# A delta-rule level product that moves all 128 columns, and a few places changed in the projections' order

## What is computed

```python
qkv, z, beta_raw, a_raw = jnp.split(h @ w_in, ...)
conv = sum over 4 taps of xp[:, j:j + T] * conv_w[j]
qkv = jax.nn.silu(conv)
q = _l2norm(q) * (DK ** -0.5);  k = _l2norm(k)
beta = jax.nn.sigmoid(beta_raw)
a = -jnp.exp(a_log) * jax.nn.softplus(a_raw + dt_bias)
b = jnp.cumsum(ac, axis=-1)
L = einsum(kc, kc) * exp(where(strict, diff, -inf)) * bc[..., :, None]
rhs = concatenate([vc * bc, kc * (bc * exp(b))])
sol = triangular_solve(L + eye, rhs, lower, unit_diagonal)
```

## Time and profile before

| | |
|---|---|
| median of 3 runs | 2790.02 us (2787.69 to 2792.81) |
| the profiled execution, own time | 2788.71 us |
| its span | 2787.1 us |
| TensorE busy (matmul) | 2654.8 us, 95% |
| VectorE, ScalarE, GpSimd busy | 1267.6, 823.5, 299.5 us |
| mean granted TensorE clock | 0.966 of full |
| chain that ended last | 86% TensorE, 7% VectorE, 3% ScalarE |

### The profile page before, as it was taken

How to read it: one execution, slowest core, us unless ns; L and a number is a source line. 1 busy time by engine, 2 the same in 40 slices (tenths; PEclk the granted TensorE clock), 3 DMA queues, 4 the chain that set the end, 5 groups by cost and what they waited for, 6 DMA issues and landing times.

```text
span 2787.1 us, 48986 instructions
## 1 busy us (share of the span) xinstructions
PE 2654.8 (95%) x20689; PEld 2550.1 (91%) x20689; DVE 1267.6 (45%) x1589; ACT 823.5 (30%) x1047; POOL 299.5 (11%) x307
## 2 busy tenths in 40 slices
PE   7999999999999999999999999989989898999997
PEld 6999998888879899999999999879988898999997
DVE  4444334636364654442344433474446645444323
ACT  3222222323232432222322222233423333322222
POOL 1000001202020210000100000004410342000000
PEclk8999999999999999999999999998899989999998
DMA  4332233424242433322433323211111111333231
GB/s 121 92 90 81 77 101 116 178 76 178 77 178 77 144 87 92 92 73 84 112 91 90 90 73 93 93 61 49 39 57 64 33 46 35 91 90 90 72 93 62
DMA packets 340961, 246.80 MB, mean 89 GB/s; under 512 B 9540, under 2 KB 322044, under 8 KB 340832
## 3 DMA queue, kind: packets, MB, share of 16 engines
q1 hardware_dynamic: 326480, 197.32, 24.1%
q0 software_dynamic: 14352, 47.58, 4.7%
HBM read 218.81 MB, written 26.05 MB: 88 GB/s over the span
## 4 chain that ended last, share of the span: by engine, by line
PE 86%; DVE 7%; ACT 3%; issue 3%; DMA 0%; POOL 0%; SPq 0%; DVEq 0%; POOLq 0%; ACTq 0%
PE ps L733 57%; PE ps L917 13%; PE ps L1103 3%; PE ps L1126 2%; PE ps L815 1%; ACT wh L1305 1%; PE ps L1113 1%; DVE wl L1610 1%; PE ps L1045 1%; PE ps L1056 1%; PE ps L824 1%; DVE cv L1929 1%; PE ps L770 1%; PE ps L1068 0%; PE ps L836 0%
## 5 line engine op out<-in xcount | busy, mean ns | idle before, releaser
L1610 DVE TENSOR_TENSOR wl<-raw,wh 128x2048 fp32r<-128x2048 f32 (+1 forms) x204 | 427.5, 2095 | 338.0 <-ACT wh L1305 337.9
L733 PE MATMUL ps<-xh,wh 128*128 128x260 f32 x2816 | 569.4, 283 | 4.9 <-DVE gate L2153 4.4
L733 PE MATMUL ps<-xh,wl 128*128 128x260 f32 x2816 | 568.6, 284 | 0.0
L733 PE MATMUL ps<-xl,wh 128*128 128x260 f32 x2816 | 567.7, 283 | 0.0
L1305 ACT ACTIVATE wh<-raw 128x2048 fp32r<-128x2048 f32 (+1 forms) x204 | 354.5, 1738 | 347.4 <-PE ps L733 212.0
L733 PEld LDWEIGHTS ps<-xh,wh 128*128 128x128 f32 x2816 | 435.9, 189 | 6.5 <-issue 5.2
L733 PEld LDWEIGHTS ps<-xh,wl 128*128 128x128 f32 x2816 | 435.4, 189 | 0.0
L733 PEld LDWEIGHTS ps<-xl,wh 128*128 128x128 f32 x2816 | 434.1, 189 | 0.0
L733 PE MATMUL ps<-hh,wh 128*128 128x260 f32 x1408 | 287.5, 286 | 13.5 <-DVE hl L2158 13.5
L733 PE MATMUL ps<-hl,wh 128*128 128x260 f32 x1408 | 285.5, 285 | 0.0
L733 PE MATMUL ps<-hh,wl 128*128 128x260 f32 x1408 | 285.4, 284 | 0.0
(11 more groups left out here) (349 smaller groups left out, 3005.5 us busy)
## 6 DMA issues: line engine op xcount, KB each, us to landing
raw<-in_ffn_gu_dram SPq DMA_DIRECT2D x176, 512.0 KB, 5.0
raw<-in_ffn_down_dram SPq DMA_DIRECT2D x64, 384.0 KB, 3.7
raw<-in_ret_w_in_dram SPq DMA_DIRECT2D x48, 512.0 KB, 4.5
raw<-in_ffn_down_dram SPq DMA_DIRECT2D x64, 320.0 KB, 4.1
s_ring<-in_state_ret_dram POOLq DMA_DIRECT2D x32, 512.0 KB, 6.5
out_dram<-s_ring POOLq DMA_DIRECT2D x32, 512.0 KB, 3.1
raw<-in_gdn_w_in_dram SPq DMA_DIRECT2D x32, 512.0 KB, 4.6
raw<-in_ret_w_out_dram SPq DMA_DIRECT2D x16, 512.0 KB, 4.2
```

Of the source, the lines that this page charges most:

```text
L733: m_ = nc.tensor.matmul(ps[:, 2 * q + h, 0:HALF], w_, v[:, kt0 + t, h * HALF:(h + 1) * HALF], start=b_, stop=e_)
L1610: nc.vector.tensor_tensor(wl[:, s, 0:cols], raw[:, s, 0:cols], wh[:, s, 0:cols].bitcast(F32), ALU.subtract).then_inc(w_low, 1)
```

## The change

Five edits, all in the delta-rule mixer. (1) `change` multiplies all 128 columns of `t1`, not the odd blocks alone, through the helper `four`; what VectorE reads of it stays the same. (2) GpSimd clears both `t1` tiles once per group, after cse2 and ahead of the stores of the conv state, so that the columns never written hold zeros. (3) The length of the eighth square (ln7) stands after unit 8 rather than 9, behind ln6, and ScalarE's root before si9 rather than behind it. (4) The product of the token decays (bcol, blast) stands after unit 6 rather than 5. (5) ScalarE's first weights split of a group stands before its wait for the turned conv state.

```diff
-LENGTH_AFTER = {n: n - 2 for n in range(2, 10)}
+LENGTH_AFTER = {**{n: [n - 2] for n in range(2, 8)}, 8: [6, 7]}
...
-    "ctc", each(4, "si", "sq"), "si4 cse0 sq4 si5 sq5 si6 sq6 si7 sq7 si8 cse1 si9 rt si10 si11 cse2",
+    "ctc", each(4, "si", "sq"), "si4 cse0 sq4 si5 sq5 si6 sq6 si7 sq7 si8 cse1 rt si9 si10 si11 cse2",
...
                 pool.wait_ge(gdn_a, A("cse2", g))
+                for ch in chain:
+                    nc.gpsimd.memset(ch["t1"][:], 0.0)
...
-                if n == 5:
+                if n == 6:
                     pe.wait_ge(pre_v, PRE_V("a", 0))
...
-                    if n in LENGTH_AFTER:
-                        lengths(LENGTH_AFTER[n])
+                    for m in LENGTH_AFTER.get(n, []):
+                        lengths(m)
...
                             act_(f"b{l - 1}.{c}")
-                        for h in range(GG):
-                            m_ = nc.tensor.matmul(blocks(ps[:, bb, h * P:(h + 1) * P], l, 1), ch["m"][:, h, :], blocks(ch["t1"][:, h, :], l, 1),
-                                                  start=True, stop=True)
-                        did(m_, f"a{l}.{c}")
+                        four(bb, ch["m"], ch["t1"], f"a{l}.{c}")
...
+                split_next(0)
                 t_("ct")
                 nc.scalar.activation(c_old[:], ps[:, 6, 0:12 * 3 * DEC], ACT.Copy).then_inc(gdn_a, A.did("ctc"))
                 for n in range(12):
-                    if n % 2 == 0:
+                    if n % 2 == 0 and n:
                         split_next(n // 2)
...
-                    if n == 9:
+                    if n == 8:
                         t_("ln7")
```

More of the change, by code:

```diff
@@ L154 @@
     "ct", " ".join(" ".join(f"bc{m} " for m in SPREAD_AFTER.get((n, 0), []))
-                   + (f"cs{TURN_AFTER[n]} " if n in TURN_AFTER else "") + (f"ln{LENGTH_AFTER[n]} " if n in LENGTH_AFTER else "")
+                   + (f"cs{TURN_AFTER[n]} " if n in TURN_AFTER else "") + " ".join(f"ln{m} " for m in LENGTH_AFTER.get(n, []))
                    + " ".join(f"bc{m}" for m in SPREAD_AFTER.get((n, 1), [])) for n in range(16)),
```

## The result

| | before | after |
|---|---|---|
| median | 2788.86 us (4 runs, 2780.96 to 2792.81) | 2761.90 us (4 runs, 2760.57 to 2767.39) |
| the profiled execution, own time | 2788.71 us | 2767.39 us |
| its span | 2787.1 us | 2765.8 us |

The ratio is 0.9908, with a 95% interval of 0.9892 to 0.9923: 27 us faster by the medians, where 26 were forecast (2764.0).

The account below looks back on a forecast made before the run. TensorE, busy 2654.8 of 2787.1 us, was taken as the bound, with its idle places and clock. 4.7 + 0 + 6.8 - 1.4 + 13.6 + 3.5 - 1.1 = 26.1 us gained, forecast 2764.0 us, range 2755 to 2777.

Parts of the forecast that it names:

- its likeliest case: The forecast itself, 2764.0 us with all its terms, was given a chance of 0.69.
- Clock in levels 4 and 6: Level loop: wider products remove eight half-clock stretches at the start of these levels, 13.6 us gained (bounds 0 and 14.4).
- Weights split: Projections of group 0: splitting ahead of ScalarE's wait starts the first turn 4.7 us earlier (bounds 0 and 5.5).
- Root and length: Projections, both groups: earlier reciprocal shortens waits for `rst` and half-clock stretches behind them, 6.8 us gained (bounds 2 and 8.7).
- Level 1: Level loop: the doubled group of eight shortens the half-clock stretches over this level, 3.5 us gained.
- Pace of 128 columns: Product `change` in the level loop: 48 groups of eight wider instructions cost 1.4 us more (0 to 2.9).
- Memsets: GpSimd ahead of the conv-state stores: VectorE's first decays in group 0 wait longer, 1.1 us lost (bounds 0 and 2.2).
- Token decays: Projections: moving their product one unit later exchanges one wait for another with the same end, 0 us (0.5 either side).

Follow-up runs that it names:

- the second set of runs: Changed kernel timed again beside the version with the root and eighth length back at their old places: 2767.60 us against 2771.36 us.
- the two kernels that share out the levels: Changed kernel with 128 columns in levels 3 and 5 only: 2760.64 us; with 128 in levels 1, 2, 4 and 6 only: 2780.15 us.
- the kernels with the late root: Changed kernel with the eighth length and the root back behind unit 9 and si9, timed twice: 2772.30 us and 2771.36 us.
- the order alone: Changed kernel with the 64-column product put back and no memsets: 2781.18 us, ratio 0.9972 to the kernel before.
- both last edits: Changed kernel with level 1's one-column products (L1058) moving 128 columns and the memsets behind the stores: 2749.17 us, ratio 0.9856 to the kernel before.

## Why the prediction was right, and where it was not

The forecast of 2764.0 us is 2.1 us from the median, and its likeliest case is the one that came: the clock in levels 4 and 6 is the largest part. That the sum came so close is partly luck. Its 26.1 us stand against 27.0 by these medians, but against 21.6 in the profiled executions and 21.5 by the medians of the second set of runs. Its terms, against the 21.6 us of the ledger:

- **Clock in levels 4 and 6, 13.6 us: right.** All eight stretches are gone, level 4 takes 6.20 us for 7.90, and the two kernels that share out the levels show that levels 3 and 5 carry it. Whether it is the number of their columns or also their layout was not separated.
- **Weights split, 4.7 us: right.** 4.7 at the first turn, 5.0 at turn 4. I said TensorE could keep no more than this because turn 4 waits for ScalarE, and it does, for 5.08 us.
- **Root and length, 6.8 us: too large; it is about 4.5 to 5.5.** The projections of both groups give 9.3 us together, of which 4.7 to 5.0 are the split's; that leaves 4.3 to 4.6, and the kernels with the late root lose 5.4 and 5.5. The waits gave what was forecast: against the late root the first spread product comes 1.8 us earlier in group 0 (1.3 in the second pair of traces) and 2.2 in group 1, where 1.9 each were worked out. They show as 1.9 us less waiting for `rst` in all and 1.3 at turn 8, which the forecast did not name; so the longest wait is still 2.8 us and not 1.9. The term that was mis-sized is the clock: both half-clock stretches behind the waits were to vanish, 4.9 us less 1.9 given back. In after the first was halved and the second stayed at the 3.4 us of before. With the late root the second is 3.3 us in one trace and 6.7 in the other, so how long it lasts is in part chance. Only with the order alone, and with both last edits, is the first one gone.
- **Stretches of the first turn and turn 4: in no term.** The split removed the half-clock stretch around the first turn. TensorE then ran at full clock and came to turn 4 sooner, where it only waited longer (5.08 us for 4.03). The stretch at turn 4 grew from 3.4 to 6.6 us, which costs about 0.7.
- **Level 1, 3.5 us gained: not borne out.** The group of eight doubled its columns inside the half-clock stretch and the clock did not come back for it. In the profiled execution 1.5 us are lost, in the second one (37.5 us of half clock) 1.7 gained. Over all traces of this study in which level 1's samples keep one column, its stretches hold 34 to 44 us with 128 columns in the product (nine traces) and 41 to 44 with 64 (three). The term cannot be told from zero.
- **Pace of 128 columns, 1.4 us: 0 in level 3.** The one-column groups behind take back what the wide ones cost, 6.10 us in both traces.
- **Memsets, 1.1 us: 0.35.** They take 1.0 us on GpSimd, but without them VectorE waits 0.76 us for TensorE's product, where it waits 1.11 with them.
- **Token decays, 0: right**, by 2762.4 against 2761.9 us.

With the sizes of the two profiled executions: 4.7 + 4.5 + 13.6 - 1.5 - 0.35 = 21.0, and 0.7 from the rest of the execution: 21.7, against 21.6. The 4.5 is what the projections leave beside the split, so that the sum closes there is no proof of it. In the prediction a root term that was too large and a level-1 gain that did not come stood beside two costs that were too large.

## What to carry to other kernels

In this kernel each product loads new weights, and beside that load up to 128 columns cost next to nothing. In levels 3 and 5 too few columns cost the clock although TensorE was never idle. So look for half-clock stretches right behind groups of narrow products, and try to widen these, with neighbouring data whose results nobody reads, before touching anything else. An edit on another engine's order is worth what the next wait leaves of it: look at which wait ends last, as at turn 4, and whether a half-clock stretch still stands behind the wait that remains. And where a single trace and a median disagree, as with the late root, compare stages and time both kernels beside each other.

## What the runs showed of the hardware that was not expected

- One column, 64 and 128 columns of float32 cost TensorE nearly the same beside their weight loads: 16 instructions with 128 columns take 1.79 us, eight with one column 0.81 to 0.87, eight with 64 columns 0.84.
- Once the clock has fallen, a doubled group inside the stretch does not bring it back: level 1 of after stays at half clock for 13.4 us in spite of eight 128-column instructions between the one-column ones. With 128 columns in all of them it stays up in three of the four pairs, and in two of four in the kernel with both edits.
- The changed kernel's median was 2761.9 us in one set of runs and 2767.6 in another, with the same code. Differences under 5 us between kernels of different sets say little here.
